# Sparse attention: gated, divided probabilities and column-tiled value products

## What is computed

```python
p_c = masked_softmax(s_c, cmp_end[None, :] <= t[:, None])     # compressed keys
o_c = jnp.einsum('bghqj,bjgd->bqghd', p_c, v_cmp)
p_s = masked_softmax(s_s, sel_pos <= t[:, None])              # selected keys
o_s = jnp.einsum('bghqn,bgqnd->bqghd', p_s, v_s)
p_w = masked_softmax(s_w, (dist >= 0) & (dist < WINDOW) & (kpos[None, :] >= 0))
o_w = jnp.einsum('bghqk,bkgd->bqghd', p_w, v_w)               # window
o = gb[..., 0:1] * o_c + gb[..., 1:2] * o_s + gb[..., 2:3] * o_w
x = x + o.reshape(B, T, 1024) @ w_out
```

## Time and profile before

| | |
|---|---|
| time, median of 3 runs | 1098.33 us (1096.89 to 1098.43) |
| span of the profiled execution | 1096.2 us |
| TensorE busy, share of the span | 1089.4 us, 99% |
| VectorE busy | 626.0 us, 57% |
| ScalarE busy | 584.0 us, 53% |
| GpSimd busy | 140.8 us, 13% |
| granted TensorE clock | 1.000 |

### The profile page before, as it was taken

How to read it: one execution, slowest core, us unless ns; L and a number is a source line. 1 busy time by engine, 2 the same in 40 slices (tenths; PEclk the granted TensorE clock), 3 DMA queues, 4 the chain that set the end, 5 groups by cost and what they waited for, 6 DMA issues and landing times.

```text
span 1096.2 us, 14109 instructions
## 1 busy us (share of the span) xinstructions
PE 1089.4 (99%) x5835; PEld 924.0 (84%) x5835; DVE 626.0 (57%) x702; ACT 584.0 (53%) x919; POOL 140.8 (13%) x203
## 2 busy tenths in 40 slices
PE   8999999999999999999999999999999999999998
PEld 6877888888999988888889888888888888888887
DVE  5544666467555445556677664455457876555442
ACT  6788655444455534347577354444447846444431
POOL 1031311110231100123320010000004400000000
PEclk9999999999999999999999999999999999999999
DMA  8843434454654554444242255544544245455551
GB/s 318 326 151 115 167 141 154 154 192 170 227 193 167 209 193 184 178 150 161 63 152 74 81 192 192 190 173 163 185 154 148 103 154 212 177 187 192 173 183 67
DMA packets 29232, 185.40 MB, mean 169 GB/s; under 512 B 3552, under 2 KB 3936, under 8 KB 9184
## 3 DMA queue, kind: packets, MB, share of 16 engines
q1 hardware_dynamic: 27344, 178.31, 45.1%
q0 software_dynamic: 1680, 5.92, 1.5%
q10 hardware_dynamic: 144, 0.26, 0.1%
HBM read 183.43 MB, written 1.05 MB: 168 GB/s over the span
## 4 chain that ended last, share of the span: by engine, by line
PE 96%; ACT 2%; DMA 1%; DVE 1%; issue 0%; SPq 0%
PE ps L593 24%; PE ps L595 24%; PE ps L596 24%; PE ps L573 6%; PE ps L708 3%; PE ps L645 3%; PE ps L646 3%; PE ps L644 3%; PE ps L730 3%; PE ps L958 1%; ACT t L1246 1%; DMA t<-in_w 1%; ACT t L1249 1%; PE ps L749 1%; PE ps L697 1%; PE ps L809 0%
## 5 line engine op out<-in xcount | busy, mean ns | idle before, releaser
L1850 DVE TENSOR_TENSOR t<-t 128x2048 fp32r<-128x2048 f32 (+7 forms) x300 | 421.1, 1418 | 333.1 <-ACT t L1249 330.5
L1249 ACT ACTIVATE t<-t 128x2048 fp32r<-128x2048 f32 (+7 forms) x258 | 338.3, 1335 | 283.3 <-PE ps L596 240.5
L593 PE MATMUL ps<-t 128*128 128x512 f32 (+2 forms) x1178 | 465.1, 395 | 0.7 <-ACT t L1249 0.7
L596 PE MATMUL ps<-t 128*128 128x512 f32 (+2 forms) x1178 | 457.4, 388 | 0.0
L595 PE MATMUL ps<-t 128*128 128x512 f32 (+2 forms) x1178 | 457.1, 388 | 0.2 <-DVE t L1850 0.2
L596 PEld LDWEIGHTS ps<-t 128*128 128x128 f32 x1178 | 221.1, 188 | 45.7
L593 PEld LDWEIGHTS ps<-t 128*128 128x128 f32 x1178 | 221.3, 188 | 44.1 <-ACT t L1249 1.3
L595 PEld LDWEIGHTS ps<-t 128*128 128x128 f32 x1178 | 221.5, 188 | 43.1 <-DVE t L1850 0.9
L2540 POOL TENSOR_TENSOR t<-t 128x32 f32<-128x32 f32 (+8 forms) x108 | 92.2, 865 | 503.3 <-ACT t L1246 448.0
L1246 ACT ACTIVATE t<-ps,t 128x256 f32<-128x256 f32 (+4 forms) x216 | 95.8, 453 | 89.1 <-DVE t L2003 46.6
L1249 ACT ACTIVATE t<-ps 128x512 fp32r<-128x512 f32 (+7 forms) x97 | 52.3, 556 | 64.7 <-PE ps L573 63.0
(11 more groups left out here) (112 smaller groups left out, 539.3 us busy)
## 6 DMA issues: line engine op xcount, KB each, us to landing
t<-in_w SPq DMA_DIRECT2D x155, 1024.0 KB, 4.9
t<-in_w SPq DMA_DIRECT2D x12, 512.0 KB, 4.3
t<-in_w SPq DMA_DIRECT2D x5, 768.0 KB, 4.1
t<-in_g POOLq DMA_DIRECT2D x4, 512.0 KB, 8.2
t<-in_w SPq DMA_DIRECT2D x2, 640.0 KB, 3.9
t<-in_w SPq DMA_DIRECT2D x4, 256.0 KB, 4.8
t<-in_x SPq DMA_DIRECT2D x1, 1024.0 KB, 7.1
t<-in_memt POOLq DMA_DIRECT2D x1, 1024.0 KB, 7.2
```

What stands on the lines that cost most here:

```text
L593: e.matmul(o, sh, wh, start=k0 + j == 0, stop=False)
L596: t = e.matmul(o, sl, wh, start=False, stop=last and j == n - 1)
L1249: return e.activation(o, src, ACT.Copy, scale=scale)
L1850: return e.tensor_tensor(o, a, b, op)
```

## The change

It makes the second block's attention like the first block's:

- VectorE's `share(u)` in lap i = u+1 takes the reciprocal of the unit's row sums and multiplies it with the gates, and `gated_rows(u)` multiplies the 512 (or 240) exponentials in `P1` with the result, in place. `turn_rows` waits for that, and comes one lap later (i-3), as does `copy_rows`.
- `weigh_columns` replaces `weigh`: values stationary, 64 columns wide, 128 turned probabilities streaming, two heads in the two column halves of one bank. All branches of (block, h) add up in that one bank, and the result is the transposed output. It is called at odd laps from 5 on for the two units i-5 and i-4.
- `join`, `turn_out` and their buffers are gone. `split` reads the attention's bank itself, in laps 26, 30, 34 and after the loop.
- Main units for h = 1 now hold two heads of one branch where they held one head of both: four score products of 256 columns where there were two of 512.
- `P1` has four buffers instead of three, `PT1` four instead of two; the loops have 36 laps instead of 35. Chunk 88's second half is multiplied ahead of the values in lap 32, chunk 89's in lap 34 (it was 33). `nwo` uses other banks. A table `WEIGHED_BY_POOL`, which would give some multiplications to GpSimd, is empty.

```diff
-    main[hg, h] = [Unit("nsa", "main", 0, h, tuple(range(u0, u0 + per)), 128 * (h + 1), hg, 2 * per, 2)
-                   for u0 in range(0, 8, per)]
+    if h == 0:
+        main[hg, h] = [Unit("nsa", "main", 0, h, (u0, u0 + 1), 128, hg, 4, 2) for u0 in range(0, 8, 2)]
+    else:
+        main[hg, h] = [Unit("nsa", "main", 0, h, (u0, u0 + 1), 256, hg, 2, 1, br) for u0 in range(0, 8, 2) for br in (0, 1)]
...
+WEIGHED_BY_POOL = ()
...
-O_BANKS = {"fox": (2, 3), "nsa": (2, 3, 2, 3, 2, 3, 0, 1, 2, 2, 2, 2), "mla": (2, 3)}
+O_BANKS = {"fox": (2, 3), "nsa": (2, 3, 0, 1), "mla": (2, 3)}
...
+    def weigh_columns(u, PT):
...
+        g, k, pt = groups_of(u)[0], O_BANKS["nsa"][NSA_GROUPS.index(groups_of(u)[0])], PT[u.i % len(PT)]
+        if u.opens:
+            take(k, "o", *g)
+        w.wait_ge(*after("off", "P", u.of, u.i))
+        at = slice((u.block * 8 + u.n[0]) // 4 * 64, (u.block * 8 + u.n[0]) // 4 * 64 + 64)
...
+        for i, (pair, v, blocks) in enumerate(products):
+            for c, z in enumerate(blocks):
+                o = bank[k][64 * c:64 * c + 64, pair * 128:(pair + 1) * 128]
+                t = e.matmul(o, v, pt[0:deep(u), z * 128:(z + 1) * 128], start=bool(u.opens) and i == 0,
+                             stop=bool(u.ends) and i == 1, skip_group_check=True)
...
-    for i in range(35):
+    for i in range(36):
-        if 2 <= i < 34:
-            turn_rows(NSA[i - 2], m.P1)
+        if 3 <= i < 35:
+            turn_rows(NSA[i - 3], m.P1)
...
-        elif i == 33:
-            turn_out(1, 0)
+        elif i == 32:
+            gemm(88, lo_out, ready_out, (1,))
+        elif i == 34:
             gemm(89, lo_out, ready_out, (1,))
-        if i in late_opens:
+        if i >= 5 and i % 2 == 1:
+            nsa_values(NSA[i - 5])
             nsa_values(NSA[i - 4])
-        if i >= 3 and i + 1 not in late_opens:
-            nsa_values(NSA[i - 3])
-        if i == 32:
-            gemm(88, lo_out, ready_out, (1,))
...
-        elif i in (25, 29):
-            turn_out(0, (i - 25) // 4)
...
+    def share(u):
+        f, gates = m.cols("sum", "nsa", u.i), m.ng[:, u.h, :].rearrange("p (n c) -> p n c", c=3)
...
+        w.wait_ge(*after("off", "s", u.of, u.i))
+        e.reciprocal(f, f).then_inc(*out(("over", u.of, u.i)))
+        w.wait_ge(*after("over", u.of, u.i))
+        w.wait_ge(*after("gates", u.h))
+        tt(own, own, gates, ALU.mult).then_inc(*out(("share", u.of, u.i)))
+
+    def gated_rows(u, P):
+        w.wait_ge(*after("share", u.of, u.i))
+        p = heads(P[u.i % len(P)][:, 0:u.rows * u.keys], u.keys)
+        tt(p, p, bc(m.cols("sum", "nsa", u.i), u.keys), ALU.mult).then_inc(*out(("normed", u.of, u.i)))
...
-        if 2 <= i < 34 and i - 2 not in TURNED_BY_ACT:
-            copy_rows(NSA[i - 2], m.PT1)
-        for n in (i - 3, i - 4):
-            if n >= 0 and (n in late_joins) == (n == i - 4):
-                for g in NSA[n].ends[:1]:
-                    join(g)
+        if 1 <= i < 33:
+            share(NSA[i - 1])
+            if i - 1 not in WEIGHED_BY_POOL:
+                gated_rows(NSA[i - 1], m.P1)
+        if 3 <= i < 35 and i - 3 not in TURNED_BY_ACT:
+            copy_rows(NSA[i - 3], m.PT1)
+        if i in (26, 30):
+            split(("o", 0, (i - 26) // 4), both(m.o_lo, 0, 4, (i - 26) // 4))
```

More of the change, by code:

```diff
@@ L246, in __init__ @@
                 self.columns["ss", name, b, h] = s[:, h * nh:(h + 1) * nh]
-        for hg in range(2):
-            for h in range(2):
-                s = self.cols("sums", hg, h, n=16)
-                for br in (1, 2):
-                    self.columns["sum", (hg, h, br)] = s[:, (br - 1) * 8:br * 8]
         ksum, qsum = self.cols("ksum", n=32), self.cols("qsum", n=32)
@@ L423, in groups_of @@
 def groups_of(u):
-    if u.kind == "main":
-        return [(u.block, u.h, 1), (u.block, u.h, 2)]
-    if u.kind == "few":
-        return [(u.block, u.h, 0)]
+    if u.of == "nsa":
+        return [(u.block, u.h)]
     return [(u.kind, u.h, u.block)]
@@ L509, in values_of @@
             out.append((groups_of(u)[0], n * 128, [(128, m.mv[:, b, n * 128:(n + 1) * 128]) for b in range(nkb)]))
-        elif u.kind == "main":
-            g = (u.block * 8 + n) // 4
-            for group, v in zip(groups_of(u), (m.vs, m.vw)):
-                out.append((group, n * 64, [(128, v[:, b, g * 64:(g + 1) * 64]) for b in range(nkb)]))
-        elif u.kind == "few":
-            out.append((groups_of(u)[0], n * 64, [(72, m.vc[:])]))
         else:
@@ L535, in maxima @@
 def maxima(m, u):
-    return m.cols("mx", u.kind, u.block, u.h, u.n[0], n=u.rows)
+    return m.cols("mx", u.of, u.i, n=u.rows)
 def sum_of(m, u, a):
-    if u.kind == "main":
-        return m.cols("sum", groups_of(u)[a % 2], n=8)[:, u.n[a // 2]:u.n[a // 2] + 1]
+    if u.of == "nsa":
+        return m.cols("sum", "nsa", u.i, n=u.rows)[:, a:a + 1]
     n = u.n[a] % 4 if u.kind == "mla" else u.n[a]
-    return m.cols("sum", groups_of(u)[0], n=8 if u.kind in ("fox", "few") else 4)[:, n:n + 1]
+    return m.cols("sum", groups_of(u)[0], n=8 if u.kind == "fox" else 4)[:, n:n + 1]
 def tensor_program(e, m, book):
@@ L1031, in ready_out @@
     def ready_out(k, h):
-        return after("off", "no", k // 4, h)
-    late_opens = [u.i + 4 for u in NSA[4:] if u.kind == "main" and u.opens and u.i < 16]
-    for i in range(35):
+        return after("off", "o", k // 4, h)
+    for i in range(36):
         if i < 32:
             nsa_scores(NSA[i])
-        if 2 <= i < 34:
-            turn_rows(NSA[i - 2], m.P1)
+        if 3 <= i < 35:
+            turn_rows(NSA[i - 3], m.P1)
         if i in (1, 2):
@@ L2229, in hidden @@
             *out(("off", ("cmpk", "cmpv")[i]), ("hidden", i)))
[L2233 to L2260 removed]
+    def share(u):
+        f, gates = m.cols("sum", "nsa", u.i), m.ng[:, u.h, :].rearrange("p (n c) -> p n c", c=3)
+        n0 = u.block * 8 + u.n[0]
+        if u.kind == "few":
+            gates, own = gates[:, n0:n0 + 4, 0], f
+        elif u.sets == 2:
+            gates, own = gates[:, n0:n0 + 2, 1:3], heads(f, 2)
+        else:
+            gates, own = gates[:, n0:n0 + 2, 1 + u.branch], f
+        w.wait_ge(*after("off", "s", u.of, u.i))
[7 more added lines that the diff above has]
+        tt(p, p, bc(m.cols("sum", "nsa", u.i), u.keys), ALU.mult).then_inc(*out(("normed", u.of, u.i)))
+    for i in range(36):
         if 1 <= i < 3:
@@ L2700, in gelu, with gated_rows @@
         tt(y, x, y, ALU.mult).then_inc(*out(("gelu", i)))
+    def gated_rows(n):
+        u = NSA[n]
+        w.wait_ge(*after("share", u.of, u.i))
+        p = heads(m.P1[u.i % len(m.P1)][:, 0:u.rows * u.keys], u.keys)
+        tt(p, p, bc(m.cols("sum", "nsa", u.i), u.keys), ALU.mult).then_inc(*out(("normed", u.of, u.i)))
+    for n in WEIGHED_BY_POOL[0:3]:
+        gated_rows(n)
     cubic(0)
     gelu(0)
+    for n in WEIGHED_BY_POOL[3:5]:
+        gated_rows(n)
     ss = m.cols("ss cmp", n=1)[0:60]
```

80 lines of the change are left out of this document (32 added, 48 removed).

## The result

| | before | changed |
|---|---|---|
| time, median of 12 runs each, on one chip | 1098.07 us (1096.62 to 1099.29) | 1099.63 us (1098.34 to 1104.73) |
| ratio | | 1.0031, 95% interval 1.0022 to 1.0040 |
| span of the profiled execution | 1096.2 us | 1098.0 us (its time 1099.82) |
| granted TensorE clock in it | 1.000 | 0.998 |

A forecast was written before the change was run, and what follows sets the result against it. TensorE was taken as the bound, VectorE becoming it in laps 17 to 30. Terms -2.1 before lap 17, -1.7 in laps 17 to 30 and -0.5 after, with rounded starts, made 3.1 us less: 1095.2 us, range 1089.5 to 1100.0.

The forecast's parts named there:

- TensorE's values, entries and scores: Attention stage on TensorE: values 10.6 us less, tiling entries 1.6 us back, h = 1 scores unchanged at 0.58 us.
- The sum of TensorE alone, -10.7: Attention stage: TensorE's own work shrinks by 10.7 us through values, entries and outputs, between -12.3 and -8.9.
- Laps 17 to 30: VectorE becomes the bound: its list of 32.9 us plus waits gives 35.0 instead of 36.7, -1.7 us.
- The waits put on top, 2.1: Laps 17 to 30: 0.15 us a lap, 2.1 us in all, for VectorE waits that no list shows.
- Before lap 17: Laps ahead of 17: TensorE saves 3.4 us, a VectorE delay costs 1.3 us, so -2.1 us.
- the forecast's -2.6 for chunk 89's first product: Around lap 31: chunk 89's first product starts at 601.5, 2.6 us earlier than before.
- 1.3 us of delay on the next maximum: Laps 4 and 5: two multiplications with shares ahead of sums and query scaling delay the next maximum 1.3 us.
- it catches up, VectorE has 11 us idle: From lap 9: VectorE, with 11 us idle in 26.4, adds some 7 to 8 and catches up.
- From lap 31 on: TensorE is the bound again after chunk 89's first product, which starts 0.61 us ahead of VectorE's lap 31; -0.5 us.
- The tail of -0.5: From chunk 89's first product on: TensorE's remaining values, turns and outputs take 0.5 us less.
- The slower one: Rival, chance 0.10: the softmax's round trip leaves 0.6 us open in each of 14 laps, giving 1101.5 us.
- The contention of GpSimd and VectorE: Shared SBUF interfaces could slow VectorE's two-input multiplications, shrinking the gain by 2.84 us to 0.3; left out of the sum.

The follow-up runs named there:

- e8: Changed kernel with VectorE's share and multiplication left out, so probabilities stay undivided and ungated: 1090.94 us, ratio 0.9937.
- e6: Changed kernel with VectorE's copy of turned rows ahead of share and multiplication in laps 3 to 16 only: 1102.22 us, ratio 1.0047.
- e15: Changed kernel with lap 5's sums and query scaling of the second head half moved ahead of share and multiplication: 1102.65 us, ratio 1.0059.
- e2: Changed kernel with VectorE's copy of turned rows ahead of share and multiplication in all laps: 1103.17 us, ratio 1.0055.
- e4: Changed kernel with the values of units 22 and 23 multiplied ahead of chunk 88's product in lap 27: 1098.54 us, ratio 1.0013.
- e13: Changed kernel with eleven multiplications on GpSimd and e4's move of lap 27's values: 1094.66 us, ratio 0.9972 to the kernel before.

## Why the prediction was wrong

- *TensorE's values, entries and scores: right but for 0.9 us.* 0.51 us a unit, entry 0.14 against 0.10, scores of h = 1 0.60 against 0.58. The Trainium skill's "TensorEngine Tiling (Array Packing)", "Overview", has a speedup of up to 2 for a dimension of at most 64; from that the estimate would be 0.42 us a unit, half of 0.84, and the trace again says 0.51.
- *The sum of TensorE alone, -10.7: mis-sized.* e8 has -6.7. Its working had no waits; the new order alone has 2.7 us of them.
- *"Laps 17 to 30", VectorE's list of 32.9 us: right, to the tenth.* From lap 17's maximum (570.35) to lap 31's (606.40) are 36.05 us, of which VectorE idles 3.17. The waits put on top, 2.1, were 3.2: -0.65 us against before instead of -1.7. The clock made the difference: the largest idle, 1.25 us, is for TensorE in the stretch at the lower clock, and in e6 and e15, which have the same order in these laps and the full clock, the same way takes 34.5 us. That is 2.2 less than before, on the good side of the forecast.
- *"Before lap 17", -2.1: the step that failed.* VectorE's lap-17 maximum came 2.7 us later (63.9 against 61.25 from lap 0), 4.8 of the 5.9 us between the forecast's -2.6 for chunk 89's first product and the measured +3.3. Without share and multiplication (e8) that maximum comes at 59.5: TensorE's saving, put at 3.4, brings 1.8 here, though the prediction's own first paragraph said that shortening TensorE alone gives nothing in laps 1 to 8. With them it comes 4.5 us later than that, and the sum had 1.3 for it. Two things were wrong in those 1.3. "1.3 us of delay on the next maximum" was near in size (1.45 at lap 6's) but named a wrong cause, as e15 shows: the part in lap 4 had the effect, the part in lap 5 none. And "it catches up, VectorE has 11 us idle" counted idle time that can't be used: it lies in front of the placing of queries, where VectorE waits for ScalarE (5.0 us in four places between 541.1 and 567.5). Relative to lap 0 the maximum of lap 9 is 1.2 us later than before and that of lap 16 is 1.1 later, so nothing was caught up. Why ScalarE came to the placing no earlier was not tested. Lap 16 of the changed kernel:

```profile
567.21 0.76 DVE L2156 SCALAR_TENSOR_TENSOR t<-ps,t 64x512 fp32r<-64x512 f32 x1 [1.30 <-ACT t L1254]
568.00 0.69 DVE L2008 TENSOR_REDUCE t<-ps 128x2 f32<-128x512 f32 x1
568.73 0.18 DVE L2249 RECIPROCAL t<-t 128x4 f32<-128x4 f32 x1
568.94 0.89 DVE L1855 TENSOR_TENSOR t<-t 128x4 f32<-128x4 f32 x2
569.75 0.68 DVE L2020 COPY t<-ps 128x512 f32<-128x512 f32 x1
570.35 0.68 DVE L2008 TENSOR_REDUCE t<-ps 128x2 f32<-128x512 f32 x1
```

  The placing starts 1.1 us later than before, relative to lap 0; and where the maxima of laps 16 and 17 were one group, share, multiplication and copy now stand between them, another 1.6 us. Those passes of lap 16 were in neither list.
- *"From lap 31 on", the product 0.61 us ahead of VectorE's lap 31: right* (605.94 and 606.40, 0.46). The tail of -0.5 was 0: from that product to the last column's end both take 31.9 us.
- *The clock was missing.* Each gap of TensorE was priced at its own length. By the timeline of lap 27, one of 1.6 us cost 3.1 in the profiled execution, and in those of e2, e6 and e15 it cost 1.6; by the twelve runs, the clock takes up to 6 us in an execution.
- *The rivals.* The slower one (the softmax's round trip, 0.6 us a lap open in laps 17 to 30) is not what happened: VectorE idled 3.2 us there, not over 4, each time for TensorE's scores, and 1101.5 was not reached by the median. One link of its circle did act, in lap 5: ScalarE waited for a maximum that stood behind a share. The contention of GpSimd and VectorE that the prediction had left out of the sum is not seen in it: VectorE's list came out exactly.

What stays open: why the clock falls in some executions and not in others of one and the same kernel, with the same waits in the same places, and whether another order of the early laps would win back the 2.5 us up to lap 8. Half of those 2.5 us are not the share's: e8 still has 1.3, with waits of 0.8 us each in laps 5 and 7.

## What to carry to other kernels

Idle time of an engine is only cover if it lies where the new work can stand: list the waits of that engine by place, and treat those that end with another engine's result as gone. When an operation is added between two others of an in-order queue, look for the pairs that stood directly one behind the other, since all that waits for the second is what becomes late. And where TensorE was without a gap, a first gap of a microsecond or two costs, in some executions, twice its length by the lower clock behind it, so cover the one or two longest waits first (e4, e13), before taking work away.
